# Two blocks on one core: transposes and value products of the attention heads moved behind later projection units

## The reference, cut to what matters

```
proj = (xn @ w_in).reshape(B, S, N_GROUPS, 3, ATTN_HEADS, ATTN_HEAD_DIM)
for g, (window, dilation) in enumerate(DIL_CONFIGS):
    q = apply_partial_rope(proj[:, :, g, 0], positions) * scale
    k = apply_partial_rope(proj[:, :, g, 1], positions)
    v = proj[:, :, g, 2]
    o, lse = dilated_window_attention(q, k, v, window, dilation)
wts = jax.nn.softmax(jnp.stack(lses), axis=0)
o = jnp.einsum('gbsh,gbshd->bshd', wts, jnp.stack(outs))
return o.reshape(B, S, ATTN_WIDTH) @ w_out
```

## Time and profile before

| what | value |
|---|---|
| median of 3 runs | 2692.99 us (2692.91 to 2693.67) |
| profiled execution | 2692.47 us |
| its span | 2690.7 us |
| PE busy | 2493.0 us, 93% of the span |
| POOL busy | 1660.8 us, 62% |
| DVE busy | 1608.9 us, 60% |
| ACT busy | 476.6 us, 18% |
| mean granted clock of PE | 0.959 |

### The profile page before, as it was taken

The page is one execution under the profiler, slowest core; times in us unless marked ns, Lnnn a source line. Parts: engine busy times, 40 slices in busy tenths (PEclk is TensorE's granted clock), DMA queues, the critical chain, the costliest instruction groups (busy, mean ns, idle before and its releaser), DMA issues.

```text
span 2690.7 us, 33885 instructions
## 1 busy us (share of the span) xinstructions
PE 2493.0 (93%) x11937; PEld 2021.9 (75%) x11937; DVE 1608.9 (60%) x1859; ACT 476.6 (18%) x904; POOL 1660.8 (62%) x700
## 2 busy tenths in 40 slices
PE   6998999997999998788888889999999998999997
PEld 4776776776878876677777778878877666887886
DVE  5767234785474467866766646444588565644456
ACT  4533222103000003111111111000032352100000
POOL 4435444674777865555555547777778323777784
PEclk8999999998999998899999999999999988999998
DMA  6212343321323321222222213323323111332331
GB/s 239 71 63 79 121 151 123 136 84 54 103 88 94 108 79 59 67 73 71 73 73 74 74 54 94 107 85 94 111 78 94 47 32 39 94 102 88 93 109 53
DMA packets 61230, 237.70 MB, mean 88 GB/s; under 512 B 7072, under 2 KB 12200, under 8 KB 57424
## 3 DMA queue, kind: packets, MB, share of 16 engines
q1 hardware_dynamic: 54720, 230.51, 26.5%
q10 hardware_dynamic: 6416, 5.95, 0.7%
HBM read 232.24 MB, written 2.10 MB: 87 GB/s over the span
## 4 chain that ended last, share of the span: by engine, by line
PE 78%; DVE 12%; ACT 3%; DVEq 2%; issue 2%; ACTq 1%; POOL 1%; DMA 1%; POOLq 0%
PE gg L533 18%; PE gg L534 17%; PE gg L535 17%; PE babcd L571 2%; PE babcd L572 2%; PE babcd L573 2%; PE gg L907 2%; PE gg L909 1%; PE gg L908 1%; DVE ta L2296 1%; DVEq L2295 1%; PE babcd L533 1%; PE babcd L534 1%; PE babcd L535 1%; DVE a_st L1699 1%
## 5 line engine op out<-in xcount | busy, mean ns | idle before, releaser
L463 POOL TENSOR_TENSOR w_hi<-raw,zero 128x1024 fp32r<-128x1024 f32 (+2 forms) x280 | 586.9, 2096 | 652.7 <-PE gg L535 476.3
L465 POOL TENSOR_TENSOR w_lo<-raw,w_hi 128x1024 fp32r<-128x1024 f32 (+2 forms) x280 | 755.4, 2698 | 39.9
L533 PE MATMUL gg<-h_hi,w_hi 128*128 128x512 f32 x1576 | 628.1, 399 | 12.1 <-ACT ff_s L1498 5.8
L534 PE MATMUL gg<-h_lo,w_hi 128*128 128x512 f32 x1576 | 621.7, 394 | 0.0
L535 PE MATMUL gg<-h_hi,w_lo 128*128 128x512 f32 x1576 | 620.6, 394 | 0.0
L533 PEld LDWEIGHTS gg<-h_hi,w_hi 128*128 128x128 f32 x1576 | 301.8, 192 | 81.5 <-issue 15.4
L535 PEld LDWEIGHTS gg<-h_hi,w_lo 128*128 128x128 f32 x1576 | 300.7, 191 | 64.1
L534 PEld LDWEIGHTS gg<-h_lo,w_hi 128*128 128x128 f32 x1576 | 301.3, 191 | 61.2
L2022 DVE TENSOR_TENSOR ta<-ff_s,gg 128x512 f32<-128x512 f32 x64 | 44.1, 689 | 332.0 <-PE gg L535 324.5
L454 POOL TENSOR_TENSOR w_hi<-raw,zero 128x1536 fp32r<-128x1536 f32 (+2 forms) x48 | 107.2, 2234 | 188.6 <-PE babcd L535 142.5
L533 PE MATMUL gg<-u_hi,w_hi 128*128 128x512 f32 x528 | 209.7, 397 | 4.2 <-issue 4.2
(11 more groups left out here) (570 smaller groups left out, 4002.5 us busy)
## 6 DMA issues: line engine op xcount, KB each, us to landing
raw<-in_w_ff_in_a SPq DMA_DIRECT2D x66, 512.0 KB, 3.6
raw<-in_w_ff_in_b SPq DMA_DIRECT2D x66, 512.0 KB, 3.6
raw<-in_w_att_qk SPq DMA_DIRECT2D x48, 512.0 KB, 3.6
raw<-in_w_ff_out_a SPq DMA_DIRECT2D x24, 704.0 KB, 4.1
raw<-in_w_ff_out_b SPq DMA_DIRECT2D x24, 704.0 KB, 4.1
late_raw<-in_w_ada SPq DMA_DIRECT2D x16, 1024.0 KB, 4.9
raw<-in_w_ml SPq DMA_DIRECT2D x25, 512.0 KB, 3.5
raw<-in_w_merge_a SPq DMA_DIRECT2D x16, 768.0 KB, 6.1
```

The source lines that it names most:

```text
L463: pool.tensor_tensor(hi, a, zero[:].to_broadcast([P, size * P]), ALU.add)
L465: pool.tensor_tensor(lo, a, hi, ALU.subtract).then_inc(S["units_split"], 1)
L533: pe.matmul(dst, w_hi[slot][:, blk], xs[0][:, k, :], start=k == 0, stop=False)
L534: pe.matmul(dst, w_hi[slot][:, blk], xs[1][:, k, :], start=False, stop=False)
```

## The change

On TensorE, the transposes of a head's probabilities are issued behind unit 5 of the next head (they were behind unit 3 in the loop, behind unit 4 for head 1). The value products are issued between the two value units (they were behind unit 4 in the loop, behind unit 5 for head 1). For head 1 the scores are issued behind unit 2 (before: 1) and the exchange behind unit 3 (before: 2).

On VectorE, `factors` in the loop stands behind the copy of unit 2, directly ahead of `norm` (before: behind the rotation of unit 1, ahead of that copy). Head 1 has an order of its own: the copies of units 0 to 2, the scores, the exchange around the copy of unit 3, the rotation of unit 0, the copy of unit 4, `factors`, `norm`, the rotation of unit 1, the copy of unit 5, and then the rotations of units 2 to 5.

```diff
-            def project_values(h):
+            def project_values(h, s):
                 u0 = FIRST["w_att"]
-                if isinstance(h, int) and h == 0:
+                if isinstance(h, int) and h == 0 and s == 0:
                     pe.wait_ge(S["att_copied"], 5)
-                wait(pe, "att_pt", h * 4)
-                for s in range(2):
-                    ready(h * 8 + (u0 + 6 + s))
-                    rows_mm((u0 + 6 + s) % 2, range(4 * s, 4 * s + 4), 384, (h_hi, h_lo), s == 0, s == 1)
+                if s == 0:
+                    wait(pe, "att_pt", h * 4)
+                ready(h * 8 + (u0 + 6 + s))
+                rows_mm((u0 + 6 + s) % 2, range(4 * s, 4 * s + 4), 384, (h_hi, h_lo), s == 0, s == 1)
...
                     att_scores(a, p)
                 if s == at_step + 1:
                     att_swap(a)
-                if s == at_step + 3:
+                if s == 5:
                     att_turn(a)
-                if s == at_step + 4:
-                    att_values(a, p)
             def att_two(i):
                 for p in range(2):
                     h = i * 2 + p
+                    first = isinstance(h, int) and h == 0
                     for s in range(6):
-                        if isinstance(h, int) and h == 0:
+                        if first:
                             first_head(s)
                             continue
                         project(h, s)
-                        att_step(h - 1, 1 - p, s, int(isinstance(h, int)))
-                    project_values(h)
+                        att_step(h - 1, 1 - p, s, 2 * isinstance(h, int))
+                    project_values(h, 0)
+                    if not first:
+                        att_values(h - 1, 1 - p)
+                    project_values(h, 1)
...
-                    a, at_step = h - 1, int(isinstance(h, int))
+                    a = h - 1
+                    if isinstance(h, int):
+                        for s in range(3):
+                            projection_out(h, p, s)
+                        score(a)
+                        swap_in(a)
+                        projection_out(h, p, 3)
+                        swap_out(a)
+                        rotate(h, p, 0)
+                        projection_out(h, p, 4)
+                        factors(a)
+                        norm(a)
+                        rotate(h, p, 1)
+                        projection_out(h, p, 5)
+                        for s in range(2, 6):
+                            rotate(h, p, s)
+                        head_out(a)
+                        continue
                     for s in range(6):
-                        if s == at_step + 1:
+                        if s == 1:
                             swap_in(a)
-                            rotate(h, p, s - 1)
+                            rotate(h, p, 0)
                         projection_out(h, p, s)
-                        if s == at_step:
+                        if s == 0:
                             score(a)
                             continue
-                        if s == at_step + 1:
+                        if s == 1:
                             swap_out(a)
-                        if s == at_step + 2:
+                        if s == 2:
+                            factors(a)
                             norm(a)
                         rotate(h, p, s)
-                        if s == at_step + 1:
-                            factors(a)
                     head_out(a)
```

## The result

The changed kernel takes 2723.86 us in the median (2720.73 to 2725.44, 4 runs), beside 2692.95 us before: a ratio of 1.0114, with a 95% interval of 1.0096 to 1.0131. It is slower by 31 us. The profiled execution has a span of 2723.6 us (before 2690.7 us), so the trace shows 32.9 us.

A forecast was written before the change was run, and what follows sets the result against it. TensorE, busy 93% of the span, was taken as the bound, so only its standstill or lower clock could be won. 2692.5 + 27 (six loop heads) + 2 (head 1) = 2721.5, forecast 2722 us, range 2714 to 2732.

The forecast's parts named there:

- P4 waits for the copy of unit 2: Loop heads: TensorE's projection unit 4 (P4) stands still 1.9 us until VectorE has copied unit 2.
- P5 waits for the copy of unit 3: Loop heads: unit 5 (P5) stands still 9.4 us; the copy follows norm and a rotation slowed by GpSimd's split.
- third rival: Loop heads: GpSimd's split also cuts norm, 2 to 4 us more in six heads, 2734 to 2746 us; chance 0.10.
- The wait of the first value unit: Behind the transposes, the first value unit newly stands still 0.95 us for all four copies.
- The transposes' wait: Loop heads: the transposes' wait for norm's scalings goes away, saving 7.72 us a head.
- The clock behind the stop: Half speed after the stop costs unit 5 1.6 us; the transposes paid this before, so both sides are equal.
- Head 1: Head 1's 7.0 us wait becomes 8.3 us, ahead of unit 2; the head ends about 2 us later (-3 to +5).
- second rival: The clock also falls ahead of the first value unit: 1.6 us more in seven heads, 2733 us; chance 0.08.
- the sum: Whole program: 2692.5 + 27 (loop) + 2 (head 1) = 2721.5 us for an execution like the profiled one.
- first rival: Loop heads: the rotation of unit 2 escapes GpSimd's split and takes 2.8 us, making the kernel faster; chance 0.10.

## Why the prediction was right

The forecast was 2722 us and slower, with 2714 to 2732 for its own mechanism; measured were 2723.9. By its steps:

- **P4 waits for the copy of unit 2**: 1.9 us forecast, 1.73 us in each of six heads. The start of P4 behind the copy was put at 0.2 us; it is 0.1 us (the copy of head 2 ends at 1187.30, P4 starts at 1187.39).
- **P5 waits for the copy of unit 3**: 9.4 us forecast; five times 9.04 and once 9.56 us. In head 2 the rotation met both parts of the split and ended 7.86 us after its start, where the forecast took 7.97 from the earlier trace rows. In head 3 it went otherwise, with nearly the same sum: the split began some 0.4 us before norm's end would have come, and its first part stopped norm instead of the first product.

```profile
1266.15 3.62 DVE L2354 TENSOR_SCALAR p_res<-p_res,a_st 128x256 f32<-128x256 f32 x4
...
1270.33 3.40 DVE L2296 TENSOR_TENSOR tb<-qk,rope_c 32x512 f32<-32x512 f32 x1
1273.81 0.68 DVE L2298 TENSOR_TENSOR ta<-ta,rope_s 32x512 f32<-32x512 f32 x1
```

The third rival priced this case too high, at 2 to 4 us a head. It came in one head of six and cost 0.5 us, since the split's two parts stop two instructions either way. That the wait is the queue's order plus GpSimd's split beside it was shown by two runs that each took one of the causes away.
- **The wait of the first value unit**: 0.95 us forecast, 0.99 us.
- **The transposes' wait** (7.5 us a head) went, as the change intends.
- **The clock behind the stop** is the term that was too small. I had set it at 1.6 us, half of the 3.1 us that the transposes took before, and equal on both sides: an estimate, which no run shows by itself. What they show is the time of each piece. Windows after, with PE's granted clock in the column behind POOL: the stop ahead of unit 5 of head 3, the two stretches of that unit, the transposes, the first value unit, and unit 5 of heads 2 and 6.

```profile
1266.70:1276.20 9.50, 0.01 (x1) 0.00 (x0) 9.08 (x9) 0.00 (x0) 6.18 (x2) 0.64 0.23 74
1276.20:1279.60 3.40, 3.33 (x8) 2.68 (x9) 2.85 (x6) 0.00 (x0) 0.00 (x0) 0.50 0.03 13
1279.60:1283.40 3.80, 3.80 (x18) 3.06 (x17) 3.16 (x6) 0.00 (x0) 0.00 (x0) 1.00 0.00 0
1283.40:1285.30 1.90, 1.82 (x16) 1.56 (x14) 1.48 (x4) 1.19 (x3) 1.57 (x1) 1.00 0.00 0
1286.20:1294.80 8.60, 8.60 (x50) 8.60 (x51) 5.33 (x3) 0.00 (x0) 4.05 (x2) 1.00 0.22 63
1202.17:1210.44 8.27, 8.27 (x25) 6.50 (x26) 6.01 (x11) 0.00 (x0) 0.00 (x0) 0.65 0.08 34
1495.16:1502.08 6.92, 6.92 (x25) 5.56 (x26) 6.02 (x11) 0.00 (x0) 0.00 (x0) 0.79 0.11 46
```

Unit 5 takes 6.92 to 8.35 us, 7.7 in the mean, against the 5.58 of the earlier trace rows: a loss of 2.1 us a head, 0.5 more than forecast. On the side of before the 1.6 us hold in the mean: the transposes took 3.1 us there and take 1.8 us now, and unit 4 behind them took 5.98 us and takes 5.73 us, since in heads 4 to 7 the lower clock lasted into that unit (0.75 to 0.83 granted in 3 us of it, where the earlier trace rows show 1.00 in head 3). So the clock costs 0.5 us more than forecast, the value units with the products take 20.1 us, not 19.9, and the waits come out 0.15 us below the forecast: 5.1 us a head, not 4.5. The loop's heads came to 73.2 us in the mean, not 72.4, and the loop to +31 us, not +27.
- **Head 1**: +2 us forecast, +1.6 us in the changed kernel and +3.2 us in the run that has it alone. The waits are those forecast, within 0.4 us. Which of the two it is hangs on the clock of the first value unit, which the prediction has in its second rival only.
- The rest: the attention starts 1.0 us earlier in this profile, and what follows the last value unit takes 1.4 us more. So the profiled execution took 2725.4 us, 3.9 more than the 2721.5 of the sum, all of it in the loop. It is the slowest of the four and lies 1.6 us over their median; that the median comes within 2 us of the forecast is in part luck.

The second rival (a lower clock ahead of the first value unit) did not come in the loop: the fourth and fifth windows above show 1.00 in the transposes and in the unit behind them, and so does the profile in the other five heads. So 1.8 us of transposes and 0.99 us of waiting did not bring the clock down in the loop.

In head 1, where the transposes come straight behind a stop of 9.5 us, it is open: the changed kernel and the run with the copy of unit 3 ahead show 1.00 in the value unit, the six other profiles with this order of head 1 show 0.50 in its first 3 us, at a price of 1.6 us. What decides between the two is not known; that the changed kernel's profile has the cheap case is luck for the term of head 1. Whether the transposes hold back the clock's rise there no run separates.

The first rival (the rotation escapes the split) needed POOL idle; I had put unit 5 at 1264.2 for it, with 6.4 us (5.5 and an estimate of 0.9 for the clock), and the program at 2688 us. The run with the split held shows what it would have been worth: 25 us, which brings the change back to 0.2% over the kernel before. It would not have been faster even then. Unit 5 starts there where I had put it (1264.3 in the times of head 3 before), but takes 8.0 us and not 6.4: that is 9 of the 11 us by which the run lies over 2688.

## What to carry to other kernels

A wait is removed only if what stands next in every queue is ready earlier; before moving work ahead, list for each engine which result the next step needs and what stands in front of it in the producer's queue. Results that free a buffer belong ahead of results that nobody waits for: here, with the transposes at the same new place, the kernel was 1.1% slower than before with the copies late and 1.5 to 1.8% faster with the copies first. Where an instruction of one engine stands still beside one of another (a product of the rotation took 3.75 us beside the second part of the split and 0.68 us alone), an order becomes a question of phase: keep the short chains that are waited for out of the long instructions of the other engine, or hold those back.

## What the runs showed of the hardware

- Scalings with a single SBUF tensor are stopped by GpSimd's instructions just as products of two tensors are (3.75 us instead of 0.68 in the changed kernel). In the run that treats head 1 alike norm's eight took 12.6 us beside four of GpSimd's instructions; they take 2.1 us without them. Each of the four stopped one scaling (the first ended at 1121.79, 0.07 us behind GpSimd's first), and one or two got through between two of them.
- An earlier stop can be cheaper than a later one: 5 us more wait ahead of unit 4 took 9 us away ahead of unit 5.
- One kernel gave 2644.3 us in one comparison and 2651.6 us in another, with ratios to the kernel before whose intervals (0.9798 to 0.9833 and 0.9839 to 0.9869) do not meet. Its heads take the same in both profiles (59.5 to 61.6 us), and the spans of the profiles differ by only 3.2 us (2646.6 and 2649.8), all of it behind the attention (the last scores start at 1528.7 and 1528.5 us). What makes the difference was not tried; differences of that size between kernels of different comparisons are left out of the conclusions above.
